# Down product of token chunks 0 and 1 as Strassen's seven block products, with block sums on GpSimd and VectorE

## The chip, the cores and the metric

The kernel runs on one core of a Trainium2 chip. Its time is in device microseconds (us), from runs of the whole program; less is better. The engines are TensorE (PE; PEld is its weight load), VectorE (DVE), ScalarE (ACT), GpSimd (POOL) and SyncE (SP, which issues the DMAs). They run their own queues in order and wait for each other by semaphores.

## The reference, cut to what matters

Two layers of a streaming encoder run over 1024 prompt tokens and 64 sample tokens with D = 1024. The end of each layer is the part that counts here:

```
def conv_ffn(x, g, w_up, conv_w, conv_b, w_down, conv_buf):
    up = rmsnorm(x, g) @ w_up
    ...
    y = (jax.nn.gelu(c[..., :D_FF], approximate=False) * c[..., D_FF:]) @ w_down
    return y, full[:, -(CONV_W - 1):]
```

D_FF is 2816, so `w_down` is 2816 x 1024. The residual is x + y. Everything is float32. The kernel keeps that precision by splitting each operand into a high part, rounded to the type fp32r, and a low part (the rest), and by three matmuls for each product: high x high, high x low, low x high (`split3`, L325).

## The kernel before, in words

Activations lie transposed in SBUF: `xT` is 128 partitions x 8 tiles of D x 1090 columns (1024 prompt tokens, 2 of padding, 64 sample tokens), cut into three chunks of 384, 384 and 322 columns (`CH`). The gate product of the up stage, `cv`, is written to DRAM (`g_scratch`) tile by tile: NF = 22 tiles f of 128 rows.

The down stage of a layer is 66 steps i, chunk by chunk (c = i // 22, f = i % 22). For a step:
- SP loads 128 rows of `w_down` (512 KB, L812) and tile f of the gates for the chunk (192 KB, L822) into places that rotate (two for raw weights, four for gates);
- ScalarE makes the high parts by a copy into fp32r (`down_high`, L1763, 1024 elements a partition; `gate_high`, L1769, 384);
- VectorE makes the low parts as raw minus high (`down_low`, L2450, and `gate_low`, L2455), both operands in SBUF;
- TensorE does 8 x 3 matmuls, one group for each of the eight 128-row tiles m of D, each into its own PSUM bank, and each bank sums over the 22 f (`step`, L1342).

After the last f of a chunk VectorE adds the eight banks into `xT` (`add_x`, L2106: one operand in PSUM, one in SBUF). ScalarE squares them and GpSimd adds the squares (`norm_add`, L375, one addition a step for the seven that a chunk needs). That is all that GpSimd does in chunks 0 and 1. In the last layer chunk 2 is done in half steps (four tiles m at a time).

The up stage ahead of it already uses Strassen-like sums of weights for its pairs p: GpSimd builds them (L2022, 512 elements), ScalarE and VectorE split them (L1721, L2330), VectorE takes the products out of PSUM (L2403), and does the convolution (L2437, L2440) and the gate product (L2445). Its last pair overlaps the start of the down stage. The raw and split weights of the first steps are prepared meanwhile.

## Time and profile before

| | |
|---|---|
| times of three runs | 2414.71, 2414.60, 2407.47 us; median 2414.6 |
| span of the profiled execution | 2412.5 us (its own time is not listed apart; the median run is 2.1 us longer) |
| TensorE clock granted, mean | 0.998 of full speed |
| chunks 0 and 1 of the down stage, layer 0 | 941.4 to 1126.9 us |
| GB/s over the span | 112 |

The span runs from the first to the last instruction. A busy TensorE does not say at what pace its matmuls follow each other, since their durations overlap; the distance of their starts does.

### The profile page before, as it was taken

Reading aid. Unit: us, or ns where it says so; the run is one execution under the profiler, and the core shown is the slowest. Engines: PE = TensorE matmul, PEld = TensorE weight load, DVE = VectorE, ACT = ScalarE, POOL = GpSimd, SP = SyncE. Lnnn points to the kernel's source line nnn. Section 1 sums busy time; section 2 is a strip of 40 time slices with the busy share of each in tenths; the row PEclk is TensorE's granted clock in tenths of the full one; section 3 lists DMA queues with packets and bytes.
Section 4 is the critical chain, followed back from the end, with each engine's and each line's share of the span. In section 5 each row is a group of like instructions: output and inputs, shape, how many; then the busy total and the mean of one; then the engine's idle time right before and its main releaser. Section 6 shows DMA issues by size and latency. Waiting matters only on the chain.

```text
span 2412.5 us, 42567 instructions
## 1 busy us (share of the span) xinstructions
PE 2388.8 (99%) x16827; PEld 2354.2 (98%) x16827; DVE 1537.0 (64%) x2697; ACT 1089.3 (45%) x2095; POOL 525.9 (22%) x578
## 2 busy tenths in 40 slices
PE   9999999999999999999999999999999999999999
PEld 8999998999999999999999999999999999999999
DVE  3115687888788876465611256877887888764454
ACT  6325676544333433343423366655333333333453
POOL 0001254432222220010110013452322222200110
PEclk9999999999999999999999999999999999999999
DMA  4442432212222223554524334321222222255564
GB/s 157 133 142 91 147 111 53 72 64 81 72 81 64 81 72 129 189 174 160 194 73 140 119 125 136 100 63 51 81 81 72 75 69 79 74 173 178 169 195 145
DMA packets 245177, 269.15 MB, mean 112 GB/s; under 512 B 16470, under 2 KB 215028, under 8 KB 242804
## 3 DMA queue, kind: packets, MB, share of 16 engines
q1 hardware_dynamic: 244980, 266.43, 34.8%
q8 instruction: 134, 2.20, 0.4%
q14 instruction: 63, 0.52, 0.1%
HBM read 216.27 MB, written 50.11 MB: 110 GB/s over the span
## 4 chain that ended last, share of the span: by engine, by line
PE 91%; issue 3%; DVE 3%; ACT 2%; POOL 1%; DMA 0%; POOLq 0%; DVEq 0%; ACTq 0%
PE bank L327 28%; PE bank L329 28%; PE bank L328 28%; PE bank L1167 1%; PE bank L1092 1%; PE bank L1137 1%; PE bank L1177 1%; PE bank L1124 0%; PE bank L1154 0%; DMA rawB<-in_w_down 0%; PE bank L1027 0%; PE bank L1032 0%; ACT wzH L1489 0%; POOL wN L1950 0%; PE bank L1184 0%
## 5 line engine op out<-in xcount | busy, mean ns | idle before, releaser
L327 PE MATMUL bank<-actH,wb 128*128 128x384 f32 (+1 forms) x1712 | 560.2, 327 | 1.4 <-DVE actL L2334 1.2
L328 PE MATMUL bank<-actL,wb 128*128 128x384 f32 (+1 forms) x1712 | 554.8, 324 | 0.0
L329 PE MATMUL bank<-actH,wb 128*128 128x384 f32 (+1 forms) x1712 | 554.6, 324 | 0.0
L327 PE MATMUL bank<-wzH,actH 128*128 128x256 f32 (+3 forms) x1296 | 369.5, 285 | 2.8 <-issue 1.5
L329 PE MATMUL bank<-wzH,actL 128*128 128x256 f32 (+3 forms) x1296 | 364.2, 281 | 0.0
L328 PE MATMUL bank<-wzL,actH 128*128 128x256 f32 (+3 forms) x1296 | 363.9, 281 | 0.0
L327 PEld LDWEIGHTS bank<-actH,wb 128*128 128x128 f32 x1712 | 322.4, 188 | 6.1 <-issue 3.2
L328 PEld LDWEIGHTS bank<-actL,wb 128*128 128x128 f32 x1712 | 323.2, 189 | 0.7
L329 PEld LDWEIGHTS bank<-actH,wb 128*128 128x128 f32 x1712 | 323.1, 189 | 0.0
L327 PEld LDWEIGHTS bank<-wzH,actH 128*128 128x128 f32 (+1 forms) x1296 | 236.3, 182 | 4.9 <-issue 2.1
L327 PE MATMUL bank<-tH,wb 128*128 128x384 f32 x704 | 237.0, 337 | 1.2 <-ACT vn L1864 1.2
L328 PE MATMUL bank<-tL,wb 128*128 128x384 f32 x704 | 236.7, 336 | 0.0
L329 PE MATMUL bank<-tH,wb 128*128 128x384 f32 x704 | 236.7, 336 | 0.0
L328 PEld LDWEIGHTS bank<-wzL,actH 128*128 128x128 f32 (+1 forms) x1296 | 236.5, 182 | 0.0
L329 PEld LDWEIGHTS bank<-wzH,actL 128*128 128x128 f32 (+1 forms) x1296 | 236.2, 182 | 0.0
L1747 ACT ACTIVATE cv<-upb,convc 128x1090 f32<-128x1090 f32 x88 | 114.5, 1301 | 241.5 <-DVE upb L2427 241.3
L2450 DVE TENSOR_TENSOR wb<-raw,wb 128x1024 fp32r<-128x1024 f32 x88 | 107.7, 1224 | 169.8 <-ACT wb L1763 169.7
L2022 POOL TENSOR_TENSOR Sf<-raw 128x512 f32<-128x512 f32 x80 | 111.0, 1388 | 387.4 <-PE bank L329 384.2
L1721 ACT ACTIVATE Sx<-Sf 128x512 fp32r<-128x512 f32 x160 | 100.5, 628 | 198.5 <-POOL Sf L2022 198.5
L1498 ACT ACTIVATE zst<-bank,stat 128x256 f32<-128x256 f32 (+3 forms) x162 | 76.1, 474 | 250.9 <-PE bank L329 250.6
L2403 DVE TENSOR_TENSOR upb<-bank,upb 128x384 f32<-128x384 f32 x280 | 148.0, 552 | 62.0 <-PE bank L329 59.1
L1763 ACT ACTIVATE wb<-raw 128x1024 fp32r<-128x1024 f32 x88 | 93.1, 1060 | 199.2 <-PE bank L329 161.5
(320 smaller groups left out, 5034.0 us busy)
## 6 DMA issues: line engine op xcount, KB each, us to landing
raw<-in_w_up SPq DMA_DIRECT2D x88, 512.0 KB, 4.4
raw<-in_w_down SPq DMA_DIRECT2D x88, 512.0 KB, 3.6
g_scratch<-cv SPq DMA_DIRECT2D x44, 545.0 KB, 3.1
rawz<-in_w_in SPq DMA_DIRECT2D x22, 1024.0 KB, 5.4
zb<-z_scratch SPq DMA_DIRECT2D x16, 1156.0 KB, 5.9
tHf<-g_scratch SPq DMA_DIRECT2D x88, 192.0 KB, 3.6
z_scratch<-zst SPq DMA_DIRECT2D x128, 128.0 KB, 1.8
raw<-in_w_out SPq DMA_DIRECT2D x128, 128.0 KB, 2.9
```

The costliest lines, as they stand in the source:

```text
L327: pe.matmul(out, aH, bH, start=first, stop=False)
L328: pe.matmul(out, aH, bL, start=False, stop=False)
L329: return pe.matmul(out, aL, bH, start=False, stop=last)
L1092: m = pe.matmul(bank[2 * hg + v][64 * c:64 * c + 64, s * 256 + k0:s * 256 + 192], bqT[q, 2 * hg + s, 64 * c:64 * c + 64], kTw[q, 64 * c + ...
L1137: m = pe.transpose(bank[2 * hg + v][:, k * P:(k + 1) * P], ends[:, (3 * v + k) * P:(3 * v + k + 1) * P], ident[:, :])
L1498: act.activation(zst[0:r, u % 3, 0:w], bank[z_bank(u)][0:r, 0:w], ACT.Gelu if u < 18 else ACT.Copy, scale=rt[0:r, t:t + 1]).then_inc(z_ev, 1)
L1721: act.activation(Sx[:, s, 0], Sf[:, s, 1], ACT.Copy).then_inc(s_h, 1)
L1747: act.activation(cv[:, :], (upb2 if h else upb1)[:, PAD:], ACT.Identity, scale=convc[:, f + 88:f + 89], bias=convc[:, f + 132:f + 133]).th ...
L1763: act.activation(h, t, ACT.Copy).then_inc(w_h, 1)
L2022: pool.tensor_tensor(Sf[:, s, 1], x, y, ALU.add if s == 0 else ALU.subtract).then_inc(s_r, 1)
L2403: dve.tensor_tensor(out, bank[b][:, 0:out.shape[1]], other, ALU.mult if i in (6, 9) else ALU.add).then_inc(take_r, 1)
L2450: dve.tensor_tensor(lo, t, h.bitcast(F32), ALU.subtract).then_inc(w_l, 1)
```

## The change

Chunks 0 and 1 (768 tokens) of the down product are taken as a 2 x 2 product of blocks: the output rows m in halves (tiles 0 to 3 and 4 to 7), the contraction in pairs of tiles f = 2j and 2j + 1 (j = 0 to 10, NJ = 11), the tokens as chunk 0 and chunk 1. The seven products run in four passes p: (0, 0) and (0, 1), (1, 0) and (1, 1), (2, 0) and (2, 1), and (3, 1) alone. A unit (p, h, j) is 4 x 3 matmuls of 384 columns into banks 4h to 4h + 3. For each unit GpSimd adds or subtracts two weight blocks of 512 elements where the product needs a sum (all but (0, 1) and (3, 1)), the two gate blocks of 384 are added on GpSimd or VectorE (five of the seven products; (2, 0) alternates), ScalarE makes the high parts, VectorE the low ones. Raw weights of all 22 tiles are loaded once, in pass 0 and 1, and kept (partly over `actH` and `actL`, which are free once the up stage's matmuls are done). Gates are loaded again in each pass. Finished products go from PSUM into one or two blocks of `xT` by additions on VectorE. `bank_free` counts them. Chunk 2 keeps its steps; what stood beside chunk 1 (squares and norms of chunk 0, splits of the next layer's weights) moves into passes 1 and 3 and into chunk 2.

The diff at its core:

```diff
+        UNITS = []
+        for p in range(3):
+            UNITS += [(p, 0, 0), (p, 0, 1), (p, 1, 0), (p, 1, 1)]
+            UNITS += [(p, h, j) for j in range(2, NJ - 2) for h in range(2)]
+            UNITS += [(p, h, j) for h in ((1, 0) if p == 2 else (0, 1)) for j in (NJ - 2, NJ - 1)]
+        UNITS += [(3, 1, j) for j in range(NJ)]
+        UNIT_NO = {u: k for k, u in enumerate(UNITS)}
+        UNIT_MM, POOL_SUM, DVE_SUM = {}, {}, {}
...
+        W_SUMS = {(0, 0): ((1, 0), (1, 1), ALU.add), (1, 0): ((0, 0), (0, 1), ALU.add), (1, 1): ((0, 1), (1, 1), ALU.subtract),
+                  (2, 0): ((0, 0), (1, 1), ALU.add), (2, 1): ((1, 0), (0, 0), ALU.subtract)}
+        W_PLAIN = {(0, 1): (1, 1), (3, 1): (0, 0)}
+        G_SUMS = {(0, 1): (1, 0, ALU.subtract), (1, 1): (0, 1, ALU.add), (2, 0): (0, 2, ALU.add), (2, 1): (0, 1, ALU.add),
+                  (3, 1): (0, 1, ALU.subtract)}
+        G_PLAIN = {(0, 0): 0, (1, 0): 1}
...
+        def g_by_pool(p, h, j):
+            return (p, h) in ((0, 1), (3, 1)) or ((p, h) == (2, 0) and j % 2 == 0)
...
+        def slot_free(l, p, h, j):
+            t = NJ * p + j
+            if t < 3:
+                return tile_mm(l, NF - 1, (2, 6, 9)[t])
+            if p < 3:
+                return unit_mm(l, (t - 3) // NJ, h, (t - 3) % NJ)
+            if j < 3:
+                return unit_mm(l, 2, *((1, NJ - 2), (1, NJ - 1), (0, NJ - 2))[j])
...
+        TARGETS = {(0, 0): ((1, 0, ALU.add), (1, 1, ALU.subtract)), (0, 1): ((0, 0, ALU.add), (1, 0, ALU.add)),
+                   (1, 0): ((0, 1, ALU.add), (0, 0, ALU.subtract)), (1, 1): ((0, 0, ALU.add),),
+                   (2, 1): ((1, 1, ALU.add),), (2, 0): ((0, 0, ALU.add), (1, 1, ALU.add)), (3, 1): ((0, 1, ALU.add), (1, 1, ALU.add))}
...
+                def load_w(t):
+                    p, j = t // NJ, t % NJ
...
+                        sp.wait_ge(mm, tile_mm(l, NF - 2, N_TILE))
+                    elif t == 2:
+                        sp.wait_ge(mm, tile_mm(l, NF - 1, N_TILE))
+                    c = slice(0, 512) if p else slice(512, 1024)
+                    for f in range(2 * j, 2 * j + 2):
+                        sp.dma_start(w_raw(f)[:, c], w_down[f * P:f * P + P, c]).then_inc(ld_in[t % 3], 16)
+                def load_gs(t):
...
+                        sp.wait_ge(w_l, max(unit_low(l, q, h, k) for h in range(2) if (q, h, k) in UNIT_NO))
+                    if t >= 3:
+                        sp.wait_ge(ld_in[t % 3], ld_at(l, t - 3))
+                    if p == 0:
+                        sp.wait_ge(g_st, (l * NF + 2 * j + 2) * 16)
...
+                    if p == 0 or p == 3:
+                        c = slice(0, 384) if p == 0 else slice(384, 768)
...
+                        return
+                    f = 2 * j + (1 if p == 1 else 0)
+                    sp.dma_start(place[:, 0:2].rearrange("p c t -> p (c t)"), g_dram[l, f, :, 0:768]).then_inc(ld_in[t % 3], 16)
+                    if p == 2:
+                        sp.dma_start(place[:, 2], g_dram[l, 2 * j + 1, :, 384:768]).then_inc(ld_in[t % 3], 16)
...
+                def unit(p, h, j):
+                    hi, lo = (w_slot(p, h, j)[:, i] for i in range(2))
+                    g = g_slot(p, h, j)
+                    pe.wait_ge(w_l, unit_low(l, p, h, j))
+                    for m in range(4):
+                        if j == 0 and p:
+                            pe.wait_ge(bank_free, product_out(l, *((0, 0), (0, 1), (1, 0), (1, 1), (2, 0), (2, 1))[2 * (p - 1) + h], m))
+                        elif j == 0 and (h == 0 or m < 2):
+                            pe.wait_ge(take_r, (l + 1) * N_TAKE - (4 * h + m < 5))
+                        elif j == 0:
+                            pe.wait_ge(row_r if m == 2 else sto_r, l + 1 if m == 2 else 2 * l + 2)
+                        s = slice(m * P, m * P + P)
+                        q = split3(pe, bank[4 * h + m][:, 0:384], hi[:, s], lo[:, s], g[:, 0], g[:, 1], j == 0, j == NJ - 1)
+                        if j == NJ - 1 or m == 3:
...
+                for p, h, j in UNITS:
+                    unit(p, h, j)
...
+                            q = pe.transpose(bank[7][0:88, s * P:(s + 1) * P],
...
+                        pe.wait_ge(bank_free, product_out(l, 2, 0, 3))
+                        norm_sum(pe, 2 * l + 2, 0)
...
+                def unit_high(p, h, j):
+                    t, u = NJ * p + j, (p, h, j)
+                    a, g = w_slot(p, h, j), g_slot(p, h, j)
+                    act.wait_ge(mm, slot_free(l, p, h, j))
+                    if (u, 0) in POOL_SUM:
+                        act.wait_ge(s_r, pool_sum(l, u, 0))
+                        src = w_slot(p, h, j, True)[:, 1]
...
+                        src = w_block(j, *W_PLAIN[p, h])
+                    act.activation(a[:, 0], src, ACT.Copy).then_inc(w_h, 1)
+                    if t in (4, 5):
+                        act.wait_ge(gmul_r, (l + 1) * NF)
+                    if (u, 1) in POOL_SUM:
+                        act.wait_ge(s_r, pool_sum(l, u, 1))
+                        src = g_slot(p, h, j, True)[:, 1]
+                    elif u in DVE_SUM:
+                        act.wait_ge(s_l, low_sum(l, u))
+                        src = g_slot(p, h, j, True)[:, 1]
+                    else:
+                        act.wait_ge(ld_in[t % 3], ld_at(l, t))
+                        src = g_raw(p, j)[:, G_PLAIN[p, h]]
...
+                for p, h, j in UNITS[4:]:
+                    unit_high(p, h, j)
+                    if (p, h) == (1, 0) and 4 <= j < 8:
+                        norm_square(act, n, 0, j, x_added(l, 0, j), j - 4)
+                    if p == 3 and 3 <= j < 7:
...
+                def unit_sums(p, h, j):
...
+                    if (u, 0) in POOL_SUM or (u, 1) in POOL_SUM:
+                        pool.wait_ge(mm, slot_free(l, p, h, j))
+                    if (u, 0) in POOL_SUM:
+                        if p < 2:
+                            pool.wait_ge(ld_in[t % 3], ld_at(l, t))
+                        x, y, op = W_SUMS[p, h]
+                        pool.tensor_tensor(w_slot(p, h, j, True)[:, 1], w_block(j, *x), w_block(j, *y), op).then_inc(s_r, 1)
+                    if (u, 1) in POOL_SUM:
+                        pool.wait_ge(ld_in[t % 3], ld_at(l, t))
+                        if t in (4, 5):
+                            pool.wait_ge(gmul_r, (l + 1) * NF)
+                        x, y, op = G_SUMS[p, h]
+                        raw_g = g_raw(p, j)
+                        pool.tensor_tensor(g_slot(p, h, j, True)[:, 1], raw_g[:, x], raw_g[:, y], op).then_inc(s_r, 1)
...
+                for p, h, j in UNITS:
+                    unit_sums(p, h, j)
+                    if (p, h) == (1, 0) and 5 <= j < 8:
+                        norm_add(pool, n, 0, j - 4)
+                    if p == 3 and 3 <= j < 7:
+                        norm_add(pool, n, 0, j + 1)
+                for c in range(1, 3):
...
+                def unit_low_parts(p, h, j):
+                    t, u = NJ * p + j, (p, h, j)
+                    a, g = w_slot(p, h, j), g_slot(p, h, j)
+                    if u in DVE_SUM:
+                        dve.wait_ge(mm, slot_free(l, p, h, j))
+                        dve.wait_ge(ld_in[t % 3], ld_at(l, t))
+                        x, y, op = G_SUMS[p, h]
+                        raw_g = g_raw(p, j)
+                        dve.tensor_tensor(g_slot(p, h, j, True)[:, 1], raw_g[:, x], raw_g[:, y], op).then_inc(s_l, 1)
+                    count = unit_low(l, p, h, j)
+                    dve.wait_ge(w_h, count - 1)
+                    src = w_slot(p, h, j, True)[:, 1] if (u, 0) in POOL_SUM else w_block(j, *W_PLAIN[p, h])
+                    dve.tensor_tensor(a[:, 1], src, a[:, 0].bitcast(F32), ALU.subtract).then_inc(w_l, 1)
+                    dve.wait_ge(w_h, count)
+                    src = g_raw(p, j)[:, G_PLAIN[p, h]] if (p, h) in G_PLAIN else g_slot(p, h, j, True)[:, 1]
+                    dve.tensor_tensor(g[:, 1], src, g[:, 0].bitcast(F32), ALU.subtract).then_inc(w_l, 1)
+                def add_product(p, h, ms=range(4)):
+                    for m in ms:
+                        dve.wait_ge(mm, unit_mm(l, p, h, NJ - 1, m))
+                        for a, c, op in TARGETS[p, h]:
+                            x = xT[:, 4 * a + m, CH[c][0]:CH[c][0] + 384]
+                            dve.wait_ge(bank_free, F0 + 3 * KT + BEFORE[p, h, m, a, c])
+                            dve.tensor_tensor(x, x, bank[4 * h + m][:, 0:384], op).then_inc(bank_free, 1)
                 def down_low(i):
...
+                for p, h, j in UNITS[4:]:
+                    unit_low_parts(p, h, j)
+                    if j == 1 and 1 <= p < 3:
+                        add_product(p - 1, h)
+                    if (p, j) == (3, 0):
+                        add_product(2, 1)
+                    if (p, j) == (3, 2):
+                        add_product(2, 0)
```

On GpSimd, the down stage of layer 0 before the change, from the last sums of the up stage (Sf) to the norms (acc and sqE are sums of squares):

```order
L2022 TENSOR_TENSOR Sf<-raw,Sf 128x512
L375 TENSOR_TENSOR acc<-acc,sqE 128x384 x9
L404 TENSOR_TENSOR stat<-stat 128x3
L375 TENSOR_TENSOR acc<-acc,sqE 128x384 x5
L375 TENSOR_TENSOR sqE<-sqE 128x322 x2
```

The same engine after the change, at the border of pass 1 and pass 2 (sAf: sums of weights, sBrf: sums of gates, grr: gates as loaded, wrA, wrB, raw, rawB: weights as loaded):

```order
L2300 TENSOR_TENSOR sAf<-wrA 128x512 x4
L2300 TENSOR_TENSOR sAf<-wrA,rawB 128x512
L2300 TENSOR_TENSOR sAf<-wrA 128x512
L2300 TENSOR_TENSOR sAf<-rawB 128x512
L2300 TENSOR_TENSOR sAf<-raw 128x512
L2307 TENSOR_TENSOR sBrf<-grr 128x384
L2300 TENSOR_TENSOR sAf<-wrB 128x512
L2300 TENSOR_TENSOR sAf<-raw 128x512
L2300 TENSOR_TENSOR sAf<-wrB 128x512
L2300 TENSOR_TENSOR sAf<-wrA 128x512
L2307 TENSOR_TENSOR sBrf<-grr 128x384
```

Where GpSimd had seven additions of squares before chunk 2 began (the first of the x9), it now has 83 block sums besides such seven.

On VectorE, steps 23 to 25 of layer 0 before the change, with the additions of chunk 0 between them:

```order
L2450 TENSOR_TENSOR wb<-raw,wb 128x1024
L2455 TENSOR_TENSOR tL<-tHf,tH 128x384
L2450 TENSOR_TENSOR wb<-raw,wb 128x1024
L2455 TENSOR_TENSOR tL<-tHf,tH 128x384
L2106 TENSOR_TENSOR xT<-bank,xT 128x384 x8
L2450 TENSOR_TENSOR wb<-raw,wb 128x1024
L2455 TENSOR_TENSOR tL<-tHf,tH 128x384
```

And after it, at the start of pass 1 (sA and sBr are the split weights and gates):

```order
L2733 TENSOR_TENSOR sBr<-grr,sBr 128x384
L2742 TENSOR_TENSOR xT<-xT,bank 128x384 x8
L2726 TENSOR_TENSOR sBrf<-grr 128x384
L2730 TENSOR_TENSOR sA<-sAf,sA 128x512
L2733 TENSOR_TENSOR sBr<-sBrf,sBr 128x384
L2726 TENSOR_TENSOR sBrf<-grr 128x384
L2730 TENSOR_TENSOR sA<-sAf,sA 128x512
L2733 TENSOR_TENSOR sBr<-sBrf,sBr 128x384
L2742 TENSOR_TENSOR xT<-xT,bank 128x384 x8
L2730 TENSOR_TENSOR sA<-sAf,sA 128x512
```

The eight additions now come twice per pass instead of once per chunk, and a unit of half a step's matmuls has its own pair of differences, with a gate sum (L2726) ahead of it where VectorE does that.

## Rows read from the trace of the kernel before

**Rows 1.** The page: busy engines (us, share, instructions) and ScalarE's copy of a sum.

```profile
PE 2388.8 (99%) x16827; PEld 2354.2 (98%) x16827; DVE 1537.0 (64%) x2697; ACT 1089.3 (45%) x2095; POOL 525.9 (22%) x578
...
L1721 ACT ACTIVATE Sx<-Sf 128x512 fp32r<-128x512 f32 x160 | 100.5, 628 | 198.5 <-POOL Sf L2022 198.5
```

**Rows 2.** Busy time by stretch: us, each engine (instructions), clock, DMA share, GB/s.

```profile
936.00:1113.00 177.00, 176.40 (x1015) 176.03 (x1014) 92.43 (x112) 73.08 (x103) 8.58 (x7) 1.00 0.53 172
```

**Rows 3.** Matmuls of L327, 930 to 1200: duration ns min/median/max, first and last start.

```profile
L327 PE MATMUL bank<-tH,wb x352: 333/336/441, 941.4 to 1126.3; 128*128 128x384 f32 x176
L327 PE MATMUL bank<-tH,wS x112: 307/312/395, 1126.9 to 1199.2; 128*128 128x322 f32 x112
```

**Rows 4.** Timeline of TensorE at 1000: start us, duration us.

```profile
1000.06 0.34 PE L327 MATMUL bank<-tH,wb 128*128 128x384 f32 x1
...
1005.82 0.34 PE L327 MATMUL bank<-tH,wb 128*128 128x384 f32 x1
```

**Rows 5.** Timelines of VectorE and ScalarE at 1010, a plain step.

```profile
1010.84 1.22 DVE L2450 TENSOR_TENSOR wb<-raw,wb 128x1024 fp32r<-128x1024 f32 x1 [2.50 <-ACT wb L1763]
1011.99 0.55 DVE L2455 TENSOR_TENSOR tL<-tHf,tH 128x384 fp32r<-128x384 f32 x1
1015.03 1.23 DVE L2450 TENSOR_TENSOR wb<-raw,wb 128x1024 fp32r<-128x1024 f32 x1 [2.49 <-ACT wb L1763]
...
1014.90 0.51 ACT L1769 ACTIVATE tH<-tHf 128x384 fp32r<-128x384 f32 x1
```

**Rows 6.** Timelines of VectorE and GpSimd in the up stage, at 700.

```profile
704.43 2.27 DVE L2440 SCALAR_TENSOR_TENSOR cv<-upb,convc,cv 128x1090 f32<-128x1090 f32 x1
...
707.95 1.22 DVE L2323 TENSOR_TENSOR wb<-raw,wb 128x1024 fp32r<-128x1024 f32 x1
709.08 2.66 DVE L2403 TENSOR_TENSOR upb<-bank,upb 128x384 f32<-128x384 f32 x5
...
712.80 1.28 DVE L2330 TENSOR_TENSOR Sx<-Sf,Sx 128x512 fp32r<-128x512 f32 x2
...
717.62 0.69 DVE L2330 TENSOR_TENSOR Sx<-Sf,Sx 128x512 fp32r<-128x512 f32 x1
...
720.82 1.34 DVE L2440 SCALAR_TENSOR_TENSOR cv<-upb,convc,cv 128x1090 f32<-128x1090 f32 x1
...
704.15 1.40 POOL L2022 TENSOR_TENSOR Sf<-raw 128x512 f32<-128x512 f32 x1 [8.71 <-PE bank L329]
708.29 2.02 POOL L2022 TENSOR_TENSOR Sf<-Sf,raw 128x512 f32<-128x512 f32 x1 [2.74 <-PE bank L329]
710.41 1.30 POOL L2022 TENSOR_TENSOR Sf<-raw 128x512 f32<-128x512 f32 x1
```

**Rows 7.** VectorE at 438, and GpSimd's norm additions of 384 over the span.

```profile
438.10 1.95 DVE L2372 TENSOR_TENSOR tLf<-actF 128x384 f32<-128x384 f32 x4
...
L375 POOL TENSOR_TENSOR acc<-acc,sqn x42: 879/1017/1685, 322.5 to 1641.4; 128x384 f32<-128x384 f32 x28, 128x322 f32<-128x322 f32 x14
```

**Rows 8.** Timeline of VectorE in the down stage, at 1036.

```profile
1035.74 1.47 DVE L2106 TENSOR_TENSOR xT<-bank,xT 128x384 f32<-128x384 f32 x3
...
1041.33 1.37 DVE L2455 TENSOR_TENSOR tL<-tHf,tH 128x384 fp32r<-128x384 f32 x1
```

**Rows 9.** Timeline of VectorE in the up stage, at 510.

```profile
511.66 1.78 DVE L2330 TENSOR_TENSOR Sx<-Sf,Sx 128x512 fp32r<-128x512 f32 x1
...
518.21 2.39 DVE L2330 TENSOR_TENSOR Sx<-Sf,Sx 128x512 fp32r<-128x512 f32 x2
```

**Rows 10.** Timeline of VectorE at 947, the last gate product of layer 0.

```profile
947.52 1.30 DVE L2445 TENSOR_TENSOR cv<-cv,cu 128x1090 f32<-128x1090 f32 x1
```

**Rows 11.** DMA issues: KB each, median us from issue to landing.

```profile
raw<-in_w_down SPq DMA_DIRECT2D x44, 256.0 KB, 3.1
```

**Rows 12.** Busy time by stretch, a mixed stage and the end.

```profile
320.00:420.00 100.00, 97.80 (x856) 90.48 (x856) 78.36 (x224) 63.73 (x206) 48.03 (x70) 1.00 0.27 80
2405.00:2412.00 7.00, 2.53 (x12) 1.95 (x11) 2.32 (x6) 1.83 (x3) 0.86 (x1) 0.50 0.52 187
```

More of the change, by code:

```diff
@@ L24 @@
 NF = FF // P
+NJ = NF // 2
 PAD = 2
@@ L351, in acc_of, with square_places @@
             return acc if n % 2 or c < 2 else sqE[:, 2]
+        def square_places(n, c):
+            return sqs[0] if n % 2 or c == 0 else sqs[1]
         def norm_square(act, n, c, m, added, q=None):
@@ new lines, in build @@
+        W_PLAIN = {(0, 1): (1, 1), (3, 1): (0, 0)}
[4 more added lines that the diff above has]
+            return (p, h) in ((0, 1), (3, 1)) or ((p, h) == (2, 0) and j % 2 == 0)
+        count = 0
+        for u in UNITS:
+            UNIT_MM[u] = count
+            count += 4 if u[2] == NJ - 1 else 1
+            if u[0:2] in W_SUMS:
+                POOL_SUM[u, 0] = len(POOL_SUM) + 1
+            if u[0:2] in G_SUMS:
+                if g_by_pool(*u):
+                    POOL_SUM[u, 1] = len(POOL_SUM) + 1
+                else:
+                    DVE_SUM[u] = len(DVE_SUM) + 1
@@ new lines, in unit_low, with ld_at @@
+        def unit_low(l, p, h, j):
+            return l * N_W + 2 * NF + 2 * UNIT_NO[p, h, j] + 2
+        def slot_free(l, p, h, j):
+            t = NJ * p + j
+            if t < 3:
+                return tile_mm(l, NF - 1, (2, 6, 9)[t])
[3 more added lines that the diff above has]
+                return unit_mm(l, 2, *((1, NJ - 2), (1, NJ - 1), (0, NJ - 2))[j])
+            return unit_mm(l, 3, 1, j - 3)
+        def ld_at(l, t):
+            mine = [(2 if k < 2 * NJ else 0) + (2 if k // NJ == 2 else 1) for k in range(t % 3, 4 * NJ, 3)]
+            return 16 * (1 + l * sum(mine) + sum(mine[0:t // 3 + 1]))
@@ L880, in _ @@
                     continue
-                for i in range(4, 3 * NF):
+                for i in range(NF):
                     load_down(i)
@@ new lines, in step @@
+                def step(f):
+                    t0, w = CH[2]
+                    h, lo = (t.rearrange("p k n -> p (k n)") for t in down_place(f)[0:2])
+                    pe.wait_ge(w_l, down_at(l, f))
+                    pe.wait_ge(b_l, gate_at(l, f))
+                    for m in range(KT):
+                        if f == 0:
+                            pe.wait_ge(bank_free, product_out(l, *((3, 1) if m >= 4 else (2, 0)), m % 4))
+                            if m == 3:
+                                pe.wait_ge(ms_r, ms_at(2 * l + 2, 0))
@@ L1850, in _ @@
                         sum_high(p + 1, 2)
-                    else:
-                        for i in range(4):
-                            gate_high(i)
                     conv_first(p, 0)
@@ L2508, in _ @@
                         weights_low(p + 1, 0)
-                    elif not ahead:
-                        down_low(0)
                     dve.wait_ge(copy_r, copy_at(l, 7 + p))
@@ L2535, in _ @@
                         sum_low(p + 1, 1)
+                    else:
+                        unit_low_parts(0, 0, 1)
                     tap(p, 0, 1)
```

459 lines of the change are left out of this document (258 added, 201 removed).

## The prediction

> **What bounds the kernel now.** I read the page first: TensorE is busy for 99% of the span, VectorE for 64%, ScalarE for 45%, GpSimd for 22% [rows 1]. The table by stretch then says this of the stage that changes (chunks 0 and 1 of the down product, layer 0): over 177 us TensorE is busy 176.4, VectorE 92.4, ScalarE 73.1, GpSimd only 8.6, at the full granted clock (1.00 of 2.4 GHz) and a DMA share of 0.53 [rows 2]. The list of the matmul line has the stage's first matmul at 941.4 and the first of chunk 2 at 1126.9 [rows 3]: 185.5 us. Matmul durations overlap, so I take the pitch: 33 matmuls of 384 columns start from 1000.06 to 1005.82, 0.1745 us each [rows 4]. A step (24 of them) is 4.19 us, which is also the distance of two steps on VectorE, 1010.84 to 1015.03 [rows 5]; 44 steps are 184.3 us, so 1.2 of the 185.5 are waits. VectorE has 2.5 us of idle time in each step [rows 5]. So fewer matmuls are worth their full pitch, as long as nobody else becomes the bound.
>
> **What is removed.** Seven block products for eight: 77 units of 12 matmuls stand where 88 half steps stood, 132 matmuls fewer in a layer, 264 in all, 46.1 us. A unit takes TensorE 12 x 0.1745 = 2.09 us, a pair of units (p, 0, j) and (p, 1, j) 4.19 us.
>
> **What is added on VectorE.** Two such instructions in a row are 0.08 us closer than their durations: two differences of 512 elements take 1.28 us, so 0.60 each [rows 6]; four of 384 elements from SBUF take 1.95, so 0.47 [rows 7]; three additions from PSUM into xT take 1.47, so about 0.46, and I use 0.47 [rows 8]. Low parts of a unit are 0.60 + 0.47 = 1.07 us, 2.14 per pair (a step cost 1.61 for the same number of matmuls: the reuse of a weight and of a gate tile over all of D is what Strassen gives up). Gate sums: 27 of 0.47 us in a layer (11 in pass 1, 11 + 5 in pass 2). Additions into xT: 48 against 16, of which 40 lie before the end of pass 3.
>
> **What is added on GpSimd.** 55 weight sums of 512 elements in a layer (11, 22, 22, 0 by pass) and 28 gate sums of 384 (11, 0, 6, 11), where it had nothing but seven additions of the norm. By themselves they take 1.30 us [rows 6] and 1.02 (the median of the norm's additions, [rows 7]), so at most 2 x 1.30 + 1.02 = 3.6 us for a pair: that would fit.
>
> **The shared piece.** It does not fit beside VectorE, and this is the term that decides. In the up stage GpSimd starts a sum at 704.15, and VectorE's L2440 of 704.43 takes 2.27 us where the one of 720.82 takes 1.34; at 707.95 VectorE has a difference under way, and GpSimd's sum of 708.29 takes 2.02 instead of the 1.30 of its next one [rows 6]. Some pairs earlier two differences take 2.39 from 518.21 where two took 1.28, and the one of 511.66 takes 1.78 where another took 0.69 [rows 6, 9]. In the down stage itself L2455 takes 1.37 where it took 0.55 [rows 5] as soon as GpSimd has a 384-element addition of the norm beside it [rows 8]. Against that the five L2403, which read PSUM and one SBUF operand, take their 2.66 us beside the sums of 708.29 and 710.41 [rows 6]. So two instructions that both read two SBUF operands exclude each other: a GpSimd sum costs VectorE 1.10 us at 512 elements (2.39 - 1.28; 1.78 - 0.69) and 0.82 at 384 (1.37 - 0.55). The Trainium skill, "SBUF — State Buffer", section "Who interferes with whom", says this of the pair of ports that the two share, with the loser blocked for the whole instruction, and that a VectorE instruction with at most one SBUF input is not in it. By its "whole instruction" each hold would be GpSimd's full 1.30 or 1.02 us, 0.2 more than the rows show, and the sum below would come out about 13 us higher in a layer; the rows decide.
>
> Hence VectorE's own work and GpSimd's holds add up, in each pass. Per pair: pass 0, 2.14 + 1.10 + 0.82 = 4.06, just under TensorE's 4.19; pass 1, 2.14 + 0.47 + 2.20 = 4.81; pass 2, 2.14 + 0.68 + 2.20 + 0.45 = 5.47; in pass 3 a unit is 1.07 + 0.82 = 1.89 against 2.09.
>
> **The sum**, from T0, the first matmul of the stage:
> - Start. The convolution of the last pair still runs on VectorE: its product ends at T0 + 7.4, as 947.52 + 1.30 is 948.8 [rows 10]. The raw weights from f = 4 on can only load from T0 (they lie over actH), landing some 3 to 4 us later (3.1 in the median for such a load, [rows 11]), and then three holds (1.10, 0.82, 1.10) fall on the taps and the product, which read two SBUF operands. Tail at T0 + 10.4, low parts of (0, 0, 2) at T0 + 11.5; TensorE has used its four prepared units at T0 + 8.4 and idles 3.1 us. It ends pass 0 at 11.5 + 18 x 2.09 = T0 + 49. VectorE ends its part at 11.5 + 17 x 1.07 + 0.82 + 7 x 1.92 = T0 + 44.
> - Pass 1: 22 x 1.07 + 11 x 0.47 + 16 additions x 0.47 = 36.2; holds 22 x 1.10 + 3 x 0.82 = 26.7. The additions read PSUM, so GpSimd may work beside them, but VectorE is right ahead of TensorE by then, GpSimd's next place comes free only when TensorE ends a unit, and TensorE waits for just these additions. I let 1.7 us of holds lie beside them. 61.2 us.
> - Pass 2: 22 x 1.07 + 16 x 0.47 + 12 x 0.47 = 36.7; holds 22 x 1.10 + 6 x 0.82 = 29.1; less 1.7. 64.1 us.
> - Pass 3: three units with 12 additions, 3.2 + 5.6 + 2.5 - 1.5 = 9.8; four with an addition of the norm each, 4 x (1.07 + 0.82 + 0.82) = 10.8; four at TensorE's pace, 8.4. 29.0 us.
> - Waits for ScalarE: behind a gate sum VectorE has one difference of 0.60 us, ScalarE's copy takes 0.51 and starts after the sum [rows 5]. Between nothing and 0.6 us for each of 27; the copy nearly fits, so I take 2 us.
>
> Together T0 + 44 + 61.2 + 64.1 + 29 + 2 = T0 + 200.3, against 185.5: 14.8 us longer in a layer, 29.6 in both. At the border to chunk 2 in layer 0, eight additions of (3, 1) at 0.94 us per output tile stand before matmuls that need 0.44 (three matmuls of 322 columns, 3 x 0.1745 x 322/384): +1.6 us. In the last layer they are spread over half steps, at nothing, behind TensorE's 1.8 us a half step; uncovered they would cost 2 us. ScalarE (0.63 and 0.51 a unit [rows 1, 5], at most 2.3 us of 4.19) and the loads (896 KB a pair in passes 0 and 1 against 704 KB a step before, so a share of 0.53 x 896/704 = 0.67) cost nothing while three places are in turn. If they failed, a unit would wait for a landing of about 4 us.
>
> Sum: +31 us. The profiled execution has a span of 2412.5 us, 2.1 below the median 2414.6 of the three runs; 2412.5 + 31 = 2443.5 as span, **2445 us** as time.
>
> **The rivals.**
> - *The additions cover the holds.* If GpSimd does its sums just while VectorE reads PSUM, all 18.8 us of the 40 additions hide holds, 13.9 more than I allow: +1 us in a layer, 2418. For it: L2403 beside GpSimd [rows 6]. Against: GpSimd is kept back by the places, as said. 0.10.
> - *Faster.* The holds fall into VectorE's waits. Some 63 us of holds a layer are charged; from 15, a quarter, the change breaks even, at a half it gives 31 - 15 = 16 a layer, about 2383; TensorE's floor (T0 + 11.5 + 73 x 2.09 = T0 + 164) is at 2373. For it: in the up stage the three differences shown keep their 0.60 to 0.69 us though GpSimd does four sums a pair [rows 6]. In pass 2 VectorE has no such time, as its own work and the holds are all of every 5.47 us. 0.11.
> - *Worse.* The queues in order hold each other up: ScalarE can't copy the next unit's weights before the gate sum of this one, and 27 waits of 0.6 us are 16 us a layer in place of 2: 2473. Holds as long as the Trainium skill's rule above has them would add 2 x 13 = 26 us and end at the same place. 0.10.
> - *The clock falls.* TensorE would be idle for a quarter of passes 1 and 2. Between 320 and 420 it loads weights for 90.5% of the time at clock 1.00, and only at the very end is 0.50 granted, with TensorE busy 2.5 of 7 us [rows 12]. At half clock a unit takes 4.2 us against 2.5 to 2.8: 10 us for every six units there, beyond 2480 soon. 0.03.
> - *It does not do what it says* is excluded: 264 matmuls are gone from TensorE's order.
>
> My forecast keeps 0.66. A difference under 0.3% (7 us) is about what a measurement of this kernel can't tell. Faster 0.11; slower 0.66 + 0.10 + 0.03 and 0.04 of the first rival, 0.83; same 0.06. Range 2418 (additions cover) to 2474 (the queues); below it the faster case, above it the clock.
>
> **What would show it.** Right: 264 matmuls fewer at an unchanged pitch of 0.1745; GpSimd's rows of 512 in the down stage mostly above 1.30 or VectorE's differences of 512 in two heaps, 0.68 and 1.8; VectorE without idle time in passes 1 and 2, TensorE waiting there for VectorE's low parts some 10 and 18 us; pass 0 near TensorE's pace; the first wait of some 3 us behind four units. Wrong: differences that keep 0.68 beside GpSimd's sums; TensorE busy 99% in passes 1 and 2; waits for DMA landings in pass 0 or 3; or waits on ScalarE's gate copies that add up to more than 5 us.

## The result, and the profile after

The changed kernel takes 2463.5 us (median of 4 runs, 2461.6 to 2465.7), the kernel before 2413.5 beside it: a ratio of 1.0213, 95% interval 1.0197 to 1.0229. That is 50 us slower, where 31 were forecast; it lies inside the range of 2418 to 2474. The profiled execution took 2465.65 us, with a span of 2463.8.

The page of the changed kernel, busy time by engine, answers to [rows 1]:

```profile
PE 2376.8 (96%) x16563; PEld 2323.9 (94%) x16563; DVE 1723.3 (70%) x2947; ACT 1116.6 (45%) x2227; POOL 765.0 (31%) x744
```

The 264 matmuls are gone, and yet TensorE's busy time falls by only 12 us and its share from 99 to 96%. Busy time by stretch shows where: the four passes of layer 0, cut at TensorE's first matmul of each (columns as in [rows 2]).

```profile
942.90:1001.50 58.60, 50.15 (x267) 49.18 (x267) 44.19 (x55) 24.29 (x46) 32.94 (x23) 0.92 0.59 193
1001.50:1066.90 65.40, 53.14 (x265) 49.51 (x265) 57.36 (x73) 24.33 (x48) 40.47 (x29) 0.94 0.44 140
1066.90:1125.20 58.30, 50.75 (x264) 47.28 (x265) 58.30 (x71) 22.95 (x45) 34.30 (x24) 0.97 0.33 103
1125.20:1153.20 28.00, 24.73 (x141) 23.76 (x140) 22.20 (x34) 12.99 (x25) 14.07 (x12) 1.00 0.56 169
```

The stage takes 210.3 us where it took 185.5 [rows 3], 24.8 more; the second layer is alike (its last unit starts 209.5 us after its first, here 208.0). In pass 2 VectorE is busy all of 58.30 us. In pass 0 nobody is: VectorE 44 of 58.6, GpSimd 33. The chain of waits between 936 and 1160 (us in all, times, longest) says for whom:

```profile
POOL sAf L2300 <- DMA wrA<-in_w_down: 34.4, 8, 8.2
DVE sA L2730 <- ACT sA L1983: 22.9, 13, 5.6
...
PE bank L397 <- DVE sBr L2733: 13.4, 11, 2.4
...
PE bank L397 <- DVE xT L2742: 11.0, 6, 4.7
```

GpSimd waits 34.4 us for raw weights, ScalarE waits for GpSimd, VectorE 22.9 us for ScalarE, and TensorE for VectorE's gate parts and for its additions. The timelines of VectorE, GpSimd, SyncE's queue and TensorE at the border from pass 0 to pass 1 show one such chain whole:

```profile
991.74 0.54 DVE L2733 TENSOR_TENSOR sBr<-grr,sBr 128x384 fp32r<-128x384 f32 x1
997.88 1.02 DVE L2730 TENSOR_TENSOR sA<-sAf,sA 128x512 fp32r<-128x512 f32 x1 [5.61 <-ACT sA L1983]
998.83 1.61 DVE L2733 TENSOR_TENSOR sBr<-grr,sBr 128x384 fp32r<-128x384 f32 x1
1000.36 1.94 DVE L2742 TENSOR_TENSOR xT<-xT,bank 128x384 f32<-128x384 f32 x4
...
995.84 1.29 POOL L2300 TENSOR_TENSOR sAf<-wrB 128x512 f32<-128x512 f32 x1 [6.72 <-PE bank L399]
...
990.17 0.33 SPq L1010 DMA_DIRECT2D grr<-g_scratch  x1
990.54 0.91 SPq L986 DMA_DIRECT2D wrB<-in_w_down  x2
...
1001.52 0.66 PE L397 MATMUL bank<-sBr,sA 128*128 128x384 f32 x1 [4.65 <-DVE xT L2742]
```

A place is one pair of tiles f in one pass, and place 12 is j = 1 of pass 1. Its weights (`wrB`) wait for no buffer (`load_w` has no wait of its own behind place 2), but they stand in SyncE's queue behind the gates of place 12, whose buffer comes free only with place 9. So they are issued at 990.54, land up to 4.7 us later (3.7 for the other), and GpSimd's sum of 995.84, ScalarE's copy and VectorE's difference of 997.88 follow. The label of GpSimd's wait names TensorE; what came last was the load. VectorE's eight additions stand behind that difference, and TensorE stands 4.65 us for a bank, until 1001.5. Inside pass 0, between its first wait and this one, TensorE's matmuls follow each other without a wait: the late loads show in TensorE's time only at the border.

The holds (what VectorE's instructions get longer by while GpSimd works) are there, but smaller than charged. VectorE's differences and sums of the stage by form (busy us, mean ns), 943 to 1153, and GpSimd's commonest sum:

```profile
L2730 DVE TENSOR_TENSOR sA<-sAf,sA 128x512 fp32r<-128x512 f32 x53 | 53.5, 1009 | 22.0 <-ACT sA L1983 22.0
L2733 DVE TENSOR_TENSOR sBr<-sBrf,sBr 128x384 fp32r<-128x384 f32 x41 | 37.8, 923 | 0.0
L2726 DVE TENSOR_TENSOR sBrf<-grr 128x384 f32<-128x384 f32 x27 | 26.5, 982 | 0.0
...
L2300 POOL TENSOR_TENSOR sAf<-wrA 128x512 f32<-128x512 f32 x41 | 62.7, 1543 | 47.5 <-DMA wrA<-in_w_down 34.4 <-PE bank L399 13.1
```

The means are 1009, 923 and 982 ns where 0.685 and 0.55 us are the unheld durations. Over all forms that is some 58 us of holds in the stage, from 86 sums and norm additions on GpSimd: near 0.67 us each.

Last, the clock: the granted clock is 0.92, 0.94 and 0.97 in passes 0 to 2. The first matmul after the first wait is at half clock, 0.69 us for 0.34:

```profile
955.77 0.69 PE L397 MATMUL bank<-sBe,sA 128*128 128x384 f32 x1 [3.23 <-DVE sBe L2733]
```

### The profile page after: what moved, and what is told of

Read it like the earlier page. It is cut to its first block, busy times and chain, and to the rows that moved or that the text cites. A ratio compares the mean times of both kernels' runs of the same rounds, so it can differ in the third digit from the quotient of the medians.

```text
span 2463.8 us, 42716 instructions
## 1 busy us (share of the span) xinstructions
PE 2376.8 (96%) x16563; PEld 2323.9 (94%) x16563; DVE 1723.3 (70%) x2947; ACT 1116.6 (45%) x2227; POOL 765.0 (31%) x744
## 4 chain that ended last, share of the span: by engine, by line
PE 70%; DVE 13%; issue 7%; DMA 3%; POOL 3%; ACT 3%; SPq 0%; DVEq 0%; POOLq 0%; ACTq 0%
PE bank L397 21%; PE bank L399 21%; PE bank L398 21%; DVE sA L2730 3%; DVE sBr L2733 3%; DVE sBrf L2726 2%; DMA wrA<-in_w_down 1%; PE bank L1373 1%; POOL sAf L2300 1%; DVE xT L2742 1%; PE bank L1298 1%; PE bank L1343 1%; DMA rawB<-in_w_down 1%; PE bank L1383 1%; DVE cv L2710 1%
## 5 line engine op out<-in xcount | busy, mean ns | idle before, releaser
L397 PE MATMUL bank<-sBr,sA 128*128 128x384 f32 x480 | 172.9, 360 | 48.4 <-DVE sBr L2733 26.3
L2707 DVE SCALAR_TENSOR_TENSOR cv<-upb,convc,cv 128x1090 f32<-128x1090 f32 x88 | 119.9, 1363 | 85.0 <-ACT cv L1962 84.3
L2358 DVE TENSOR_TENSOR wzL<-rawz,wzH 128x2048 fp32r<-128x2048 f32 (+1 forms) x24 | 55.0, 2291 | 175.7 <-ACT wzH L1704 170.4
L398 PE MATMUL bank<-sBr,sA 128*128 128x384 f32 x480 | 167.9, 350 | 0.0
L399 PE MATMUL bank<-sBr,sA 128*128 128x384 f32 x480 | 167.4, 349 | 0.0
```

The lines of the kernel that those rows point to most:

```text
L397: pe.matmul(out, aH, bH, start=first, stop=False)
L398: pe.matmul(out, aH, bL, start=False, stop=False)
L399: return pe.matmul(out, aL, bH, start=False, stop=last)
L2358: dve.tensor_tensor(wzL[s % 2][:, :, 0:w], rawz(s, l)[:, :, 0:w], wzH[s % 2][:, :, 0:w].bitcast(F32), ALU.subtract).then_inc(wz_l, 1)
L2707: dve.scalar_tensor_tensor(cv[:, :], t[:, 1:1 + TC], convc[:, f + 44:f + 45], cv[:, :], ALU.mult, ALU.add).then_inc(tap_r, 1)
```

## The experiments

All times are medians, beside runs of the kernel before on the same chip, whose median was 2412.5 to 2413.7 us; each ratio is to those.

**1. GpSimd copies instead of sums.** Each sum on GpSimd becomes a copy of its first operand, so the second block is left out of every such sum.

```
-  pool.tensor_tensor(w_slot(p, h, j, True)[:, 1], w_block(j, *x), w_block(j, *y), op).then_inc(s_r, 1)
+  pool.tensor_copy(w_slot(p, h, j, True)[:, 1], w_block(j, *x)).then_inc(s_r, 1)
   (and the same for the sums of the gates)
```

> Every block sum that GpSimd makes in the Strassen stage is replaced by a copy of its first operand: same tiles, same places, same waits, but one SBUF input where there were two (so the output is not the reference's). Theory A, the hold: a GpSimd sum with two SBUF inputs keeps VectorE's two-input differences waiting, some 58 us a layer in the changed kernel, and one with a single input does not. Then VectorE's 512-element differences come back from about 0.98 to 0.69 and 0.55 us, VectorE is no longer full in pass 2 (58.30 of 58.3 us before this edit), and the stage falls by 25 to 35 us a layer from 210.3: 2400 to 2415 us. Theory B, the load chain: what holds the stage is that the raw weights of three places on are loaded only after the gates of this place, and VectorE's sums merely fill time that it would wait anyway. Then the differences may get short, but the stage falls by less than 12 us a layer: 2440 us or more, with GpSimd's waits for weight loads still over 30 us a layer.

Measured: 2391.0 us, ratio 0.9905 (0.989 to 0.9919): 72.5 us under the changed kernel, and 9 under the range of theory A. The same forms of VectorE, and GpSimd's copy:

```profile
L2730 DVE TENSOR_TENSOR sA<-sAf,sA 128x512 fp32r<-128x512 f32 x53 | 40.3, 761 | 21.6 <-ACT sA L1983 21.6
L2733 DVE TENSOR_TENSOR sBr<-sBrf,sBr 128x384 fp32r<-128x384 f32 x41 | 26.8, 653 | 0.0
...
L2300 POOL COPY sAf<-wrA 128x512 f32<-128x512 f32 x44 | 34.8, 803 | 71.1 <-PE bank L399 33.0 <-DMA wrA<-in_w_down 32.5 <-DMA rawB<-in_w_down 5.4
```

What GpSimd does there costs far more than the load chain, whose wait of 32.5 us is still there. But the mean durations are 761 and 653 ns, not 685 and 550: some 19 us of holds are left, 0.23 us for each of 79 copies and seven norm additions. That the copies have a part in it is seen where no norm addition runs, in pass 2 (VectorE, then GpSimd):

```profile
1065.17 0.96 DVE L2726 TENSOR_TENSOR sBrf<-grr 128x384 f32<-128x384 f32 x1
1066.05 0.68 DVE L2730 TENSOR_TENSOR sA<-sAf,sA 128x512 fp32r<-128x512 f32 x1
1066.72 0.56 DVE L2733 TENSOR_TENSOR sBr<-sBrf,sBr 128x384 fp32r<-128x384 f32 x1
1067.20 0.97 DVE L2726 TENSOR_TENSOR sBrf<-grr 128x384 f32<-128x384 f32 x1
...
1064.78 0.94 POOL L2300 COPY sAf<-wrA 128x512 f32<-128x512 f32 x1 [1.02 <-PE bank L399]
1066.90 0.85 POOL L2300 COPY sAf<-wrA 128x512 f32<-128x512 f32 x1 [1.18 <-PE bank L399]
```

The two sums that start beside a copy take 0.96 and 0.97 us, where such a sum takes 0.55 alone: a GpSimd copy with one SBUF input holds VectorE too.

**2. Two copies for each sum.** The copy shortens GpSimd's turn as well, so this run gives the length back (the edit in short; `dst`, `x` and `spare` stand for longer names).

```
+  pool.tensor_copy(dst, x).then_inc(spare, 1)
+  pool.wait_ge(spare, ...)
   pool.tensor_copy(dst, x).then_inc(s_r, 1)
```

> The run with copies in place of GpSimd's sums took away two things at once: the second SBUF input, and half of each sum's length on GpSimd (0.80 us for the copy of 512 elements, 1.54 for the sum). Here each sum is two such copies in a row, the second behind a wait for the first, so that GpSimd works about as long as with the sums, and still has one SBUF input at a time (the output is again not the reference's). Theory A, the hold: VectorE's differences stay at 0.65 to 0.85 us, and the time is 2390 to 2402 us. Rival, GpSimd's latency: what the copies gave back was the shorter chain of load, sum, high part and low part; then the time goes back over 2435 us.

Measured: 2432.1 us, ratio 1.0077 (1.0062 to 1.0093). Neither expectation: 31 us under the changed kernel, 41 over the single copy. VectorE's differences of 512 (53 of them) now take 923 ns on the mean, and over all forms the holds are some 42 us, 0.26 for each copy. So the reasoning "one SBUF input, no hold" was wrong. How long GpSimd works counts, as twice the copies hold twice as much. The second input counts as well: GpSimd is busy 134 us in this stage and 122 in the changed kernel, and holds 42 us here and 58 there. The run can't say how much of the 41 us is hold and how much the later sum; experiment 7 takes the hold by itself.

**3. All sums on VectorE.** The first four units' sums stay on GpSimd. VectorE makes the sums of the next unit ahead of this one's differences.

```
-  for p, h, j in UNITS[4:]:
+  sums(*UNITS[4])
+  for k, (p, h, j) in enumerate(UNITS[4:], 5):
+      if k < len(UNITS):
+          sums(*UNITS[k])
       unit_low_parts(p, h, j)
```

> All block sums of the stage but those of its first four units move from GpSimd to VectorE, which makes the sums of the next unit ahead of the differences of this one. Theory A, the hold: a GpSimd sum costs VectorE about 1.1 us (512) or 0.8 us (384) of holding, and making it itself costs 0.60 or 0.47. VectorE then needs 3.2, 3.8 and 4.3 us a pair in passes 0, 1 and 2 against TensorE's 4.19, the stage takes 170 to 180 us where it takes 210.3, and the time is 2390 to 2410 us. Rival A2, the work: the hold is small beside the sums themselves, and VectorE, already full in pass 2, gets some 50 us more of work a layer: the stage takes 225 us or more and the time is 2490 or more. Theory B, the load chain: passes 0 and 1 keep their 58.6 and 65.4 us, since what they wait for is weights, and the time stays above 2440.

Measured: 2418.0 us, ratio 1.0015 (1.0006 to 1.0024). 45.5 us of the 50 are back, in one move that gives VectorE 79 more instructions a layer. By form, 943 to 1153:

```profile
L2744 DVE TENSOR_TENSOR sA<-sAf,sA 128x512 fp32r<-128x512 f32 x53 | 36.3, 685 | 0.9 <-ACT sA L1985 0.9
L2728 DVE TENSOR_TENSOR sAf<-wrA 128x512 f32<-128x512 f32 x41 | 28.5, 696 | 2.9 <-DMA wrA<-in_w_down 2.7
L2747 DVE TENSOR_TENSOR sBr<-sBrf,sBr 128x384 fp32r<-128x384 f32 x41 | 23.3, 569 | 0.0
```

Hardly anything is held, VectorE hardly waits, and its busy time in the stage is 169.8 us of 186.0 where it was 182.1 of 210.3. Moving the sums away had cost VectorE more than making them. But of the 24.3 us that the stage gets shorter only 12.3 are busy time of VectorE; the other 12.0 are its idle time, mostly for ScalarE's copies of sums (22.9 us in the changed kernel, 0.9 here). So this run doesn't show the hold alone; experiment 7 does. The result is 8 us above the range that I gave to theory A: TensorE still stands at the borders (the first unit of pass 2 comes 5.81 us after the one before, a plain one 2.12), and pass 3 takes 29.9 us. There TensorE waits 2.8 us for a low part that stands in VectorE's queue behind eight additions, and VectorE waits 4.5 us in all for gate loads.

**4. Weight loads issued early.** Two places further ahead, on semaphores of their own.

```
+  load_w(4)
+  load_w(5)
   for t in range(4, 4 * NJ):
       load_gs(t)
-      if t < 2 * NJ:
-          load_w(t)
+      if t + 2 < 2 * NJ:
+          load_w(t + 2)
```

> The loads of the raw down weights are issued two places further ahead of the gates' loads and signal on semaphores of their own, so that they no longer wait for the buffers of the gates; nothing else is changed. Theory B, the load chain: GpSimd's waits for weight loads (40 us a layer) fall under 10, VectorE's wait for the chain of load, sum and high part goes from 28 us to about 12, and the time falls by 10 to 15 us a layer, to 2435 to 2445. Theory A, the hold alone: VectorE stays the bound in passes 1 and 2, whose lengths stay 65 and 58 us within 3, and the time stays above 2455.

Measured: 2442.8 us, ratio 1.012 (1.0103 to 1.0137): 20.7 us under the changed kernel. Waits between 936 and 1160, and passes 0 to 2 by stretch:

```profile
DVE sA L2739 <- ACT sA L1992: 9.1, 7, 2.5
POOL sAf L2309 <- DMA wrA<-in_w_down: 8.9, 1, 8.9
```

```profile
941.20:993.70 52.50, 48.91 (x268) 47.86 (x267) 49.54 (x56) 24.97 (x46) 34.60 (x23) 0.97 0.71 235
993.70:1057.70 64.00, 52.14 (x266) 48.29 (x265) 58.29 (x72) 24.10 (x48) 42.82 (x29) 0.94 0.40 127
1057.70:1116.30 58.60, 53.28 (x264) 50.06 (x265) 58.60 (x71) 22.97 (x45) 34.01 (x24) 0.92 0.33 102
```

Pass 0 falls from 58.6 to 52.5 us, and pass 1 starts without a wait: the 4.65 us for a bank are gone. Passes 1 and 2 keep their lengths within 1.5 us. So the load chain is a cost of its own, and it lies in pass 0 and at its end. At the border to pass 2 the wait for a bank stays, 4.23 us where it was 4.24, so there it isn't the loads. The stage is 7.0 us shorter in the first layer and, from its first to its last matmul, 8.5 in the second (203.0 for 211.5); where the rest of the 20.7 us lies is open.

**5. Additions early**, alone and with the loads.

```
-  if j == 1 and 1 <= p < 3:
+  if j == 0 and 1 <= p < 3:
       add_product(p - 1, h)
```

> VectorE adds a finished product to x right behind the first unit of the same half of the next pass, where it did so behind the second. Theory C, the place of the additions: TensorE's waits of 4.7 us at the starts of passes 1 and 2 for freed banks fall to 1.5 us or less each, and the time falls by about 6 us a layer: 2448 to 2454. Theory A: VectorE is full behind the border, so what TensorE gains at the border it waits for a unit or two later, and the time stays within 3 us of 2463.

> The early weight loads and the early additions together, with the sums left on GpSimd. If the two waits are separate terms, they add: 21 and 6 us below the changed kernel, 2436 to 2439. If VectorE is the bound behind them, what the one gives the other cannot give again: 2441 to 2446. In both cases the passes 1 and 2 stay over 60 and 56 us, because the hold stays.

Measured: alone 2457.9 us, ratio 1.0184 (1.0168 to 1.02), 5.6 us less than the changed kernel and between the two expectations. The wait of 4.65 us for a bank is gone, and one unit later TensorE waits 1.94 us for low parts, then 2.36 us for a bank:

```profile
997.32 0.44 PE L397 MATMUL bank<-sBr,sA 128*128 128x384 f32 x1 [1.94 <-DVE sBr L2733]
1002.07 0.41 PE L397 MATMUL bank<-sBr,sA 128*128 128x384 f32 x1 [2.36 <-DVE xT L2742]
```

With the early loads 2447.0, ratio 1.0137 (1.0123 to 1.0151): no less than with the early loads alone, where the sum of the two effects would be 2436 to 2439. (It is 4 us more, but the intervals of the two ratios overlap.) They don't add. Behind the first border TensorE now waits 1.81 and 1.82 us for low parts, where with the early loads alone it had one wait of 2.37 us for a bank: VectorE is the bound there, and additions in front of the low parts delay these. This agrees with the second expectation, slightly beyond its range.

**6. TensorE kept busy at the borders.** 18 transposes of a constant ahead of the first unit of passes 1 and 2. At the first border they take 2.13 us of the wait, and 1.91 us of it are left.

> Ahead of the first units of passes 1 and 2 TensorE makes 18 transposes of a constant into unused columns, which fill its wait of 4.7 us there; nothing else is changed but that VectorE's additions of the second product wait for the first unit behind them. Theory D, the clock: the units behind the border, 4.0, 3.0 and 3.3 us in the changed kernel, go back to 2.1, and the time falls by 3 to 5 us a layer, to 2453 to 2458. Theory A, the hold: VectorE gives the units' low parts no sooner, so that TensorE waits where it was slow, and the time stays within 3 us of 2463.

Measured: 2464.1 us, ratio 1.0208 (1.0194 to 1.0222), no change. The stretches of the border and of the first unit behind it, first in the changed kernel, then here:

```profile
994.60:1001.50 6.90, 2.26 (x13) 1.96 (x12) 3.62 (x5) 1.67 (x3) 5.66 (x4) 0.84 0.34 128
1001.50:1005.50 4.00, 3.98 (x13) 3.94 (x14) 4.00 (x9) 0.84 (x2) 1.31 (x2) 0.50 0.00 0
```

```profile
991.10:997.30 6.20, 4.29 (x33) 4.04 (x31) 3.69 (x5) 1.68 (x3) 5.73 (x5) 1.00 0.35 128
997.30:1000.60 3.30, 2.94 (x13) 1.99 (x13) 3.30 (x8) 0.19 (x1) 1.27 (x2) 1.00 0.02 5
```

The granted clock stays at 1.00 where it had been 0.50, and the units behind take 3.3 us, waiting for VectorE's additions, where they took 4.0 at half clock. The clock fell behind the waits, and cost nothing that VectorE didn't take anyway. Counted from the first matmul of the pass, the third unit starts at 6.95 us in both runs in pass 1 and at 7.51 in both in pass 2: what the first unit gains is waited for again. (The run's other edit, by which the additions of the second product wait for the first unit, delays nothing at the first border: VectorE begins them at 1003.07, right behind its instruction before.) The same can't be said of the two slow units behind TensorE's first wait (4.00 and 3.01 us for 2.12): no filler was tried there, since all eight banks are accumulating.

**7. Everything together, and then GpSimd busy for nobody.** Experiments 3, 4 and 5 in one kernel, and for pass 3 the gate loads released by VectorE's sums and the third product's additions spread over four units.

> All together: sums on VectorE, early weight loads, early additions, and in pass 3 the gate loads released by VectorE's sums and the additions of the third product spread over four units. Theories A, B and C as terms that add: from the 2418 us of the run with the sums on VectorE, some 3 us a layer at the start and the two borders come off in each, and 3 in pass 3: 2400 to 2408 us, which is under the kernel before (2413.5). Rival: VectorE has no room left at the borders (the 48 additions cost 0.47 us each wherever they stand), so early additions only push the low parts back: 2412 or more.

Measured: 2399.5 us (5 runs), ratio 0.9939 (0.9926 to 0.9951): 64 us under the changed kernel, 14 under the one before, and half a us under the range expected. The stage by stretch:

```profile
941.10:989.90 48.80, 47.21 (x269) 46.57 (x268) 43.63 (x80) 23.87 (x45) 0.00 (x0) 1.00 0.77 253
989.90:1040.80 50.90, 48.37 (x265) 46.02 (x265) 48.01 (x89) 24.68 (x48) 13.14 (x3) 1.00 0.50 159
1040.80:1092.50 51.70, 49.87 (x264) 46.92 (x265) 51.70 (x99) 23.57 (x45) 0.00 (x0) 0.97 0.42 126
1092.50:1121.60 29.10, 25.67 (x144) 24.19 (x143) 27.46 (x48) 13.52 (x26) 4.70 (x4) 1.00 0.53 162
```

180.5 us against 185.5 before the change. With this as a ground, GpSimd gets additions in the places of its old sums that nobody reads or waits for:

```
+  if (u, s) in DVE_SUM and (s == 0 or g_by_pool(p, h, j)):
+      spare_op(lambda: pool.tensor_tensor(junk[:, :], junk[:, :], junk[:, :], ALU.add))
```

> The kernel with everything together, and beside it on GpSimd, in the places where the changed kernel had its sums, one addition of 344 elements with SBUF inputs only, into a spare tile of zeros that nothing reads and nobody waits for. The output is the reference's. Theory A, the hold: GpSimd's instructions cost VectorE time by merely running beside its two-input ones. Some 75 of them a layer at 0.5 to 0.9 us (the sums of 384 and 512 elements cost 0.66 on the mean in the changed kernel) are 38 to 68 us, of which VectorE has 10 free in the stage: 28 to 58 us more a layer, 2455 to 2515 us. Rival, latency: GpSimd's sums cost only through those who wait for them; then nothing changes, 2395 to 2405 us.

Measured: 2462.1 us, ratio 1.0207 (1.0191 to 1.0222): 62.6 us for work that nothing depends on. The stage by stretch:

```profile
943.00:994.70 51.70, 49.37 (x268) 47.36 (x267) 50.96 (x79) 24.27 (x45) 28.07 (x22) 0.97 0.75 239
994.70:1061.20 66.50, 51.90 (x267) 47.19 (x265) 63.49 (x90) 25.22 (x48) 40.18 (x31) 0.97 0.38 122
1061.20:1113.50 52.30, 51.56 (x265) 49.31 (x265) 52.30 (x100) 23.57 (x45) 41.69 (x3) 0.91 0.41 125
1113.50:1154.10 40.60, 27.70 (x143) 25.08 (x143) 37.68 (x48) 13.72 (x25) 31.36 (x33) 0.96 0.37 116
```

In pass 1 VectorE is busy 63.5 us for 48.0, with one instruction more: 15.5 us of pure holds from 28 more instructions on GpSimd, 0.55 each. Pass 2 is the other face of it: there VectorE has no gap, GpSimd starts three instructions in 52 us, and the pass loses only 0.6. What was held back comes in pass 3, which takes 11.5 us more, with VectorE busy 10.2 us more. ScalarE also waits 9.7 us there for the norm's additions, which stand behind the spare ones in GpSimd's queue; whether any of the 11.5 us comes from that is not shown.

**8. The order on VectorE.** As 7, with a unit's sums right ahead of its own differences.

> The kernel with everything together, with one thing undone: VectorE makes a unit's sums right ahead of the same unit's differences, and not one unit ahead. Theory E, the order counts: between a sum and the difference of its low part ScalarE must copy the high part (0.6 us), so VectorE waits about half a microsecond in most of the 74 units; some 37 us less what is free in the stage, about 10, are 15 to 27 us a layer: 2430 to 2453 us. Rival: the sum of the gates covers ScalarE's copy of the weights' sum, and VectorE loses less than is free: 2397 to 2408 us.

Measured: 2440.1 us, ratio 1.0117 (1.01 to 1.0134), 40.7 us more than in 7. VectorE's difference of a summed block, 943 to 1120:

```profile
L2756 DVE TENSOR_TENSOR sA<-sAf,sA 128x512 fp32r<-128x512 f32 x53 | 36.7, 693 | 24.7 <-ACT sA L1997 24.7
```

It waits 24.7 us for ScalarE, 0.76 behind a single sum and 0.29 where a gate sum stands between. So the order on VectorE is worth nearly as much as taking the sums off GpSimd.

## Why the prediction was right in its sign and 19 us short

**Right, by its own steps.** The matmuls went, the pitch rose only from 2.09 to 2.12 us a unit in passes 0 to 2 (2.08 in the first units of pass 3). The first wait was forecast at 3.1 us and measured at 3.23; pass 3 at 29.0, measured 28.0. Passes 1 and 2 together, with the 2 us for ScalarE, were to take TensorE from T0 + 49 to T0 + 171.3, 122.3 us; they took 123.7, and 122.6 with the early loads. GpSimd's sums of 512 take 1543 ns on the mean, above 1.30, as said, and in pass 2 VectorE is never idle.

**The step that failed** is "the loads cost nothing while three places are in turn". Pass 0 was forecast at 49 us and took 58.6. Of the 9.6 us, 4.65 are TensorE's wait for a bank at the end; some 2.8 are two units at half clock behind the first wait; that wait ended 1.4 us later than forecast (T0 + 12.9 for T0 + 11.5); most of the rest is the pitch. (That is where TensorE's time went. With the loads early, in experiment 4, 3.5 of the 9.6 us are left.) The share of DMA time that I worked out was right enough (0.67 forecast, 0.59 measured), and it was the wrong question: the loads weren't short of bandwidth, they were issued late, in one queue behind a wait for the gates' buffer. Experiment 4 takes exactly this away, and brings the time to 2442.8 us, against the forecast of 2445. Most of the 10 us that the stage took beyond the forecast (210.3 for 200.3) is in this pass. The late load kept the eight additions back and with them TensorE's bank, a wait that the sum had nowhere. The prediction named this case (a unit that waits about 4 us for a landing, and waits for landings in pass 0 as a sign of being wrong), but gave it no total and no chance.

**Right in kind, wrong in size: the holds.** 1.10 and 0.82 us a sum were taken from single pairs in the up stage. In pass 1 VectorE's own work was forecast at 36.2 us and it was busy 57.4, so 21.2 us of holds where 25.0 were charged; in pass 2 36.7 and 58.3, so 21.6 where 27.4 were. Some of GpSimd's instructions run while VectorE waits or reads PSUM. So the holds of the two passes were 9.6 us smaller than charged, and in pass 1 VectorE was idle for 8.0 us, waiting for ScalarE and behind it for GpSimd's sums, where the forecast had 2 us: two errors cancelled, and that passes 1 and 2 came out on the forecast is luck. And "two instructions that both read two SBUF operands exclude each other" was too narrow: GpSimd copies with one input hold VectorE as well (experiments 1 and 2). The Trainium skill, "SBUF — State Buffer", section "Who interferes with whom", asks only that the GpSimd instruction read SBUF while VectorE's has two SBUF inputs, which is more than the prediction took from it; the runs with copies agree.

**Smaller terms.** At the border to chunk 2 in layer 0 the sum has 1.6 us, and TensorE waits 0.4 us there. That the time lies in the range is in part luck too: the upper end, 2474, was set by waits for ScalarE behind gate sums, which did not come.

**The clock.** The rival "the clock falls" was given 0.03, in the form that time goes beyond 2480. The clock did fall, to 0.50 in stretches of 4 us, but experiment 6 shows that at the borders it cost nothing. What it costs behind the first wait, up to 2.8 us a layer, stays open.

**The other rivals.** "The additions cover the holds" and "faster" are out with the holds above. "The queues in order" in its first form is out too: VectorE's differences of the weights do wait for ScalarE, but for the chain behind ScalarE, and the waits fell from 22.9 to 9.1 us when only loads moved.

**Where the forecast should have gone further.** That the holds bound the stage was in the prediction; what follows from it was not: a sum that VectorE makes itself costs it 0.60 or 0.47 us, less than the hold (1.10 and 0.82 as charged, 0.67 on the mean as measured). Experiments 3 and 7 turn that, and the shorter chain, into 2418 and 2399.5 us.

## What to carry to other kernels

Before work goes from VectorE to GpSimd because GpSimd is idle, compare two numbers from the trace: what the instruction costs VectorE if it does it itself, and by how much VectorE's neighbours with two SBUF inputs get longer while GpSimd works. Here the second was larger (0.67 us as measured, against 0.56, an estimate for the mean of the 79 sums from 0.60 and 0.47), and work that nobody waited for cost 63 us. Count the way through the other queue as well: half of what the stage won by taking the sums back was waiting.

For each load ask not only whether its bandwidth is there but what stands ahead of it in its queue: a load that is free to go, issued behind one that must wait for a buffer, is as late as that one. And a fast path through several engines needs its order: a sum that is one unit early was worth 41 us here.
